# Rotated queries of the last attention turned through memory, query roots on GpSimd, and scores kept as three triangles side by side

## The reference

```python
def odd_mixer(h, w_in, q_norm_w, k_norm_w, sinks, w_out, pos):
    proj = h @ w_in
    q, k, v, gate = split(proj)            # 2048, 256, 256, 2048 columns
    q = rope(rms_norm_2(q as 32 heads of 64, q_norm_w), pos)
    k = rope(rms_norm_2(k as 4 heads of 64, k_norm_w), pos)
    o = swa_sinks(q, k, v, sinks)
    return (o * silu(gate)) @ w_out

def swa_sinks(...):                        # block = window = 128 tokens
    scores = q . k / 8                     # a block of queries sees its own and the previous block of keys
    band = (key <= query) & (query - key < 128)
    m = max(max(scores in the band), sink)
    p = exp(scores - m);  p = p / (sum(p) + exp(sink - m))
    return p @ v
```

## Time and profile before

| | |
|---|---|
| median of three runs | 1881.83 us |
| the profiled execution, its own time | 1880.64 us |
| its span | 1878.8 us |
| TensorE busy in the span | 1873.9 us (100%) |
| VectorE, ScalarE, GpSimd busy | 1255.8 us, 996.6 us, 14.4 us |
| granted clock of TensorE | 1.00 over the span |
| mean of the DMA | 200 GB/s |

### The profile page before, as it was taken

One profiled execution on the slowest core, in us unless ns is written; L12 is line 12 of the kernel. 1 busy time (PEld: TensorE's weight loads), 2 busy tenths in 40 slices (PEclk: granted clock), 3 DMA queues, 4 the chain that ended last, 5 costly groups with the idle time before them and its releaser, 6 DMA issues.

```text
span 1878.8 us, 22394 instructions
## 1 busy us (share of the span) xinstructions
PE 1873.9 (100%) x8531; PEld 1543.7 (82%) x8531; DVE 1255.8 (67%) x1837; ACT 996.6 (53%) x1370; POOL 14.4 (1%) x32
## 2 busy tenths in 40 slices
PE   9999999999999999999999999999999999999999
PEld 7888888888888888888888888888888888877777
DVE  6676566776666556665466776765776666778875
ACT  6677554554444344443444455564565555566763
POOL 0001000000000000000000000000000000000000
PEclk9999999999999999999999999999999999999999
DMA  9767764786666666666666696666666577656555
GB/s 320 207 196 176 207 183 150 217 254 195 193 193 193 195 192 191 191 199 192 191 196 193 207 280 196 193 191 190 191 200 194 194 239 236 183 160 186 174 186 178
DMA packets 212363, 375.96 MB, mean 200 GB/s; under 512 B 14673, under 2 KB 35969, under 8 KB 212257
## 3 DMA queue, kind: packets, MB, share of 16 engines
q1 hardware_dynamic: 211008, 371.78, 65.3%
q0 software_dynamic: 816, 2.11, 0.9%
q10 hardware_dynamic: 432, 0.66, 0.1%
HBM read 361.89 MB, written 12.60 MB: 199 GB/s over the span
## 4 chain that ended last, share of the span: by engine, by line
PE 100%; DVE 0%; issue 0%; DVEq 0%
PE g L1223 32%; PE g L1225 32%; PE g L1224 32%; PE m L1157 1%; PE ob L1302 0%; PE m L1284 0%; PE m L1384 0%; PE m L1282 0%; PE m L1165 0%; PE ob L1305 0%; PE m L1269 0%; PE ob L1370 0%; PE m L1314 0%; PE m L1335 0%; PE g L1211 0%; PE g L1210 0%
## 5 line engine op out<-in xcount | busy, mean ns | idle before, releaser
L1694 DVE TENSOR_TENSOR wl<-raw,wh 128x1024 fp32r<-128x1024 f32 (+1 forms) x660 | 802.3, 1217 | 544.9 <-ACT wh L1414 542.0
L1414 ACT ACTIVATE wh<-raw 128x1024 fp32r<-128x1024 f32 (+1 forms) x661 | 695.0, 1053 | 717.3 <-PE g L1225 709.5
L1223 PE MATMUL g<-wh,xh 128*128 128x512 f32 x1886 | 740.9, 393 | 0.1
L1225 PE MATMUL g<-wh,xl 128*128 128x512 f32 x1886 | 734.5, 389 | 0.0
L1224 PE MATMUL g<-wl,xh 128*128 128x512 f32 x1886 | 734.1, 389 | 0.0
L1223 PEld LDWEIGHTS g<-wh,xh 128*128 128x128 f32 x1886 | 354.1, 188 | 78.1 <-issue 3.9
L1225 PEld LDWEIGHTS g<-wh,xl 128*128 128x128 f32 x1886 | 354.0, 188 | 74.2
L1224 PEld LDWEIGHTS g<-wl,xh 128*128 128x128 f32 x1886 | 354.2, 188 | 72.1
L1223 PE MATMUL g<-wh,mh 128*128 128x512 f32 x732 | 287.6, 393 | 0.0
L1225 PE MATMUL g<-wh,ml 128*128 128x512 f32 x732 | 285.1, 389 | 0.0
L1224 PE MATMUL g<-wl,mh 128*128 128x512 f32 x732 | 284.9, 389 | 0.0
(11 more groups left out here) (186 smaller groups left out, 757.5 us busy)
## 6 DMA issues: line engine op xcount, KB each, us to landing
raw<-in_ev_w_in SPq DMA_DIRECT2D x128, 512.0 KB, 3.9
raw<-in_w_in SPq DMA_DIRECT2D x92, 512.0 KB, 4.3
raw<-in_w_gate SPq DMA_DIRECT2D x88, 512.0 KB, 4.5
raw<-in_w_up SPq DMA_DIRECT2D x88, 512.0 KB, 4.4
raw<-in_w_down SPq DMA_DIRECT2D x88, 512.0 KB, 4.7
raw<-in_od_w_in SPq DMA_DIRECT2D x72, 512.0 KB, 4.2
raw<-in_w_out SPq DMA_DIRECT2D x32, 512.0 KB, 4.2
raw<-in_ev_w_out SPq DMA_DIRECT2D x32, 512.0 KB, 4.7
```

Of the source, the lines that this page charges most:

```text
L1223: e.matmul(o, hi[:, kt, c], h, start=first, stop=False)
L1225: last = e.matmul(o, lo[:, kt, c], h, start=False, stop=end)
L1414: return e.activation(o, i, AF.Copy, scale=scale)
L1694: return e.tensor_tensor(o, a, b, op)
```

## The change

1. **Queries through memory.** `oq_turn` is gone. In its place stand `turn`, `send` and `fetch` of `("qsent", j, k)`: VectorE transposes `T3[:, k]` (128x512) in blocks of 32x32, SyncE's queue writes it with four DMAs and reads it back with four more, each 128 partitions of four runs of 32 numbers, straight into `qo`. `oqk` waits on TensorE for both fetches.
2. **Query roots on GpSimd.** `on_root j` is 14 instructions of 128x16 on GpSimd; `omax` waits for them.
3. **Three triangles.** The scores of a head keep their 384 columns. VectorE adds a band of 384 columns in one instruction; the maximum is two reductions in place of one; the second exponential has 256 columns; `oapt g 2` turns the third part of all four heads, so there are 12 transposes a group in place of 8, and nothing is taken apart behind them.
4. **Costs and order.** The table `WORK`, the gates of the lanes (`og` waits until an `ogate` is placed) and so the order from the keys of this layer on.

```diff
-        "oqk": (0, 2.9, 1.75), "omax": (0, 1.6, 0), "oexp": (1.17, 0, 0), "oapt": (.62, .84, .45), "oapv": (.6, 0, 1.6),
+        "oqk": (0, 2.2, 1.75), "omax": (0, 2.25, 0), "oexp": (1.28, 0, 0), "oapt": (.62, 0, .45), "oapv": (.6, 0, 1.6),
...
-            for k, p in enumerate(("on_sum", "on_root")):
-                yield 2 if k else 1
-                yield from self.made("on_rope", a[0], k)
-                say("oq_turn", a[0], k)
+                if k:
+                    self.sent_in_place(a[0], 0)
+            yield 1
+            yield from self.room("dve", 1.0)
+            self.sent_in_place(a[0], 1)
+            for p in ("on_sum", "on_root"):
+                yield 1
                 yield from self.room("dve", 1.0)
                 say(p, a[0])
...
+    def sent_in_place(self, j, k):
+
+        p = ("qsent", j, k)
+        self.say("turn", *p)
+        self.say("send", *p)
+        self.place[p], self.before[p] = ("q", 0), None
+        self.turns.append(p)
+        self.spawn(self.fetched_in_place(p))
+
+    def fetched_in_place(self, p):
+
+        yield 4
+        self.say("fetch", *p)
+        self.end[("fetch",) + p] = self.now + 4.6
+        yield 1
...
                 elif kind == "oqk":
                     g, j = a[0], a[0] // 2
-                    on.wait_ge(*moved("oq_turn", j, 1))
+                    for k in range(2):
+                        on.wait_ge(*back(("qsent", j, k)))
...
-                    tiles = [(h, c) for h in (2 * i, 2 * i + 1) for c in range(2)]
+                    tiles = [(h, c) for h in (2 * i, 2 * i + 1) for c in range(2)] if i < 2 else [(h, 2) for h in range(4)]
...
-                    for kb in range(2):
-                        c = od_probs(g)[:, i, 128 * kb:128 * kb + 128]
-                        last = e.activation(c, c, AF.Exp, bias=mx[:, h, kb:kb + 1],
...
+                    for kb, (lo, hi) in enumerate(((0, 128), (128, 384))):
+                        last = e.activation(od_probs(g)[:, i, lo:hi], od_probs(g)[:, i, lo:hi], AF.Exp, bias=mx[:, h, kb:kb + 1],
...
-                            own[i] = steps.mark(tt(od_probs(g)[:, i, :], od_bank(g, i)[:, 0:256], C("band", 0, 256), ALU.add))
...
-                            e.copy_predicated(od_probs(g)[:, n, 128:256], C("band", 256, 384).bitcast(i32),
-                                              od_bank(g, n)[:, 256:384]).then_inc(s_bank_dve if n < 3 else s_ob_dve, 1)
...
+                        tt(od_probs(g)[:, i, :], od_bank(g, i)[:, 0:384], C("band"), ALU.add).then_inc(s_bank_dve if i < 3 else s_ob_dve, 1)
...
-                    on.wait_ge(s_root, roots[("on_root", g // 2)])
+                    on.wait_ge(s_qroot, g // 2 + 1)
...
-                    stt(PO[2][:, 256 * i:256 * i + 256].rearrange("p (h t) -> p h t", h=2), both, -1.0, low, ALU.mult,
-                        ALU.mult)
-                    stt(both, low, 1.0, both, ALU.add, ALU.mult).then_inc(s_masked, 1)
...
+                elif kind == "on_root" and a[0] != "k":
+                    on.wait_ge(s_on_sum, nth(*p))
+                    if a[0]:
+                        on.wait_ge(s_qroot, a[0])
+                    yi = py_.bitcast(i32)
+                    on.wait_ge(*steps.mark(e.tensor_scalar(pv_, rsq[a[0]], 64e-6, None, ALU.add)))
...
+                    rows_ = memory[n % 4].rearrange("p (i n) -> p i n", i=4)
+                    if a[0] == "qsent":
+                        for i in range(4):
+                            e.dma_start(to[:, :, 32 * i:32 * i + 32], rows_[:, i].rearrange("p (m n) -> p m n", m=4)
+                                        ).then_inc(s_fetch[n % 4], 16)
```

More of the change, by code:

```diff
@@ L187, in say @@
         self.end[p] = max(self.through[x] for x, n in (("act", act), ("dve", dve)) if n) if act + dve else self.now
+        if p[0] == "on_root" and p[1] != "k":
+            self.end[p] = max(self.end[("on_sum", p[1])], self.now) + 4.2
         if p[0] in ("xturn", "mix", "hmix", "cmix", "xsent", "msent"):
@@ L419, in after @@
             assert kind == "og"
+            while a[0] >= 2 and ("ogate", 2 * a[0] - 3) not in self.said:
+                yield 1
             yield from self.room("act", .6)
@@ L506, in od_heads @@
         for g in (2 * j, 2 * j + 1):
-            while g >= 2 and ("oapt", g - 2, 1) not in self.said:
+            while g >= 2 and ("oapt", g - 2, 2) not in self.said:
                 yield 1
@@ L513, in od_quad @@
         say = self.say
+        while ("fetch", "qsent", g // 2, 1) not in self.said:
+            yield 1
         for _ in range(8):
-            if (all(self.end[p] <= self.now for p in [("oq_turn", g // 2, 1)] + self.ring[-3:] +
+            if (all(self.end[p] <= self.now for p in [("fetch", "qsent", g // 2, 1)] + self.ring[-3:] +
                     [self.ob] * (g > 0)) and
@@ L536, in od_quad @@
         yield 1
-        yield from self.made("oapt", g, 1)
+        say("oapt", g, 2)
+        yield 1
+        yield from self.made("oapt", g, 2)
         while g >= 2 and ("msent", "M5", 2 * g - 4, "o", g - 2) not in self.said:
@@ L723, in program @@
     sents = {p: n + 1 for n, p in enumerate(q for q in plan.order if q[0] in ("xsent", "msent"))}
-    assert plan.turns == [q[1:] for q in plan.order if q[0] == "turn"] == list(sents)
+    assert plan.turns == [q[1:] for q in plan.order if q[0] == "turn"]
+    assert [p for p in plan.turns if p[0] != "qsent"] == list(sents)
+    turned_n = {p: n + 1 for n, p in enumerate(plan.turns)}
     ropes = {p: n + 1 for n, p in enumerate(q for q in plan.order if q[0] == "eq_rope")}
@@ L1050, in sent @@
         def sent(p):
-            n = sents[p] - 1
+            n = turned_n[p] - 1
             return s_send[n % 2], 64 * (n // 2 + 1)
         def back(p):
-            n = sents[p] - 1
-            return s_fetch[n % 4], 16 * (n // 4 + 1)
+            n = turned_n[p] - 1
+            return s_fetch[n % 4], sum(64 if q[0] == "qsent" else 16 for q in plan.turns[n % 4:n + 1:4])
         def last_sent(*start):
@@ L1278, in tensor @@
                             on.wait_ge(*bank_free("oqk", g, n))
-                        heads = [(od_bank(g, n), qo[rows_of(n), j % 2, 2 * (g % 2) + n // 2, :],
+                        heads = [(od_bank(g, n), [qo[rows_of(n), j % 2, k, 2 * (g % 2) + n // 2] for k in range(2)],
                                   ko[rows_of(n), j, :]) for n in (i, i + 1)]
                         for o, q, k in heads:
-                            e.matmul(o[:, 0:128], q[:, 0:128], k[:, 0:128], start=True, stop=True)
+                            e.matmul(o[:, 0:128], q[0], k[:, 0:128], start=True, stop=True)
                         for n, (o, q, k) in enumerate(heads):
-                            e.matmul(o[:, 128:384], q[:, 128:256], k[:, 0:256], start=True,
+                            e.matmul(o[:, 128:384], q[1], k[:, 0:256], start=True,
                                      stop=True).then_inc(s_pv if i + n == 3 else s_bank, 1)
@@ L2232, in gpsimd @@
                     e.memset(K.rearrange("p (c t) -> p c t", t=128)[:, :, 0:1], 0.0).then_inc(s_g_one, 1)
+                elif kind == "on_root" and a[0] != "k":
[4 more added lines that the diff above has]
+                    on.wait_ge(*steps.mark(e.tensor_scalar(pv_, rsq[a[0]], 64e-6, None, ALU.add)))
+                    on.wait_ge(*steps.mark(e.tensor_scalar(yi, pv_.bitcast(i32), -0.5, 1597463007.0, ALU.mult, ALU.add)))
+                    for i in range(3):
+                        on.wait_ge(*steps.mark(e.tensor_tensor(pq_, pv_, py_, ALU.mult)))
+                        on.wait_ge(*steps.mark(e.tensor_tensor(pq_, pq_, py_, ALU.mult)))
+                        half, more = (-0.5, 1.5) if i == 2 else (-0.5, 1.5)
+                        on.wait_ge(*steps.mark(e.tensor_scalar(pq_, pq_, half, more, ALU.mult, ALU.add)))
+                        if i < 2:
+                            on.wait_ge(*steps.mark(e.tensor_tensor(py_, py_, pq_, ALU.mult)))
+                    e.tensor_tensor(rsq[a[0]], py_, pq_, ALU.mult).then_inc(s_qroot, 1)
                 elif kind == "dec":
```

117 lines of the change are left out of this document (49 added, 68 removed).

## The result

| | before | the change |
|---|---|---|
| median of 14 runs each, side by side | 1881.03 us | 1885.61 us |
| lowest and highest | 1880.32 to 1882.14 | 1883.30 to 1887.24 |
| the profiled execution, its own time | 1880.64 us | 1883.64 us |
| its span | 1878.8 us | 1881.8 us |
| VectorE, ScalarE, GpSimd busy | 1255.8, 996.6, 14.4 us | 1243.5, 999.9, 35.2 us |

The ratio is 1.0025, 95% interval 1.0018 to 1.0032: slower by 4.6 us, a little beyond the 0.2% that the prediction named. One thing must be known to read the profile: its execution ran at a mean granted clock of 1.000, as only two of the fourteen did (1883.64 and 1883.30 us). The other twelve had 0.998 or 0.999 and took 1885.04 to 1887.24.

A forecast was written before the change was run, and what follows sets the result against it. The prediction took TensorE alone, busy 50.00 of 50 us, to bound the kernel. TensorE's work summed to 0 and the fetch stall to 1.5 us, so 1881.8 + 1.5 = 1883.3 us, range 1880.8 to 1887.8.

The forecast's parts named there:

- TensorE's own work: Last attention: eight turns of queries go, eight of probabilities come, 0.44 us each, 3.5 us either way; sum 0.
- VectorE, costed at 0: Last attention: about 18 us less work on an engine off the path; at most it removes 1.0 us of waits.
- The sum of -18: VectorE's net: -13.4 for the groups, -9.9 for four roots gone, +5.7 for eight block transposes.
- ScalarE: Last attention: 32 exponentials double from 128 columns, about 0.1 us each, 3 us over 200; nothing on the path.
- GpSimd's root: 14 instructions ahead of a group's maximum take 2.5 to 11 us, hidden behind five units of 13.6 us.
- The way of the queries through memory: First scores wait for the fetched queries of block 0: a stall of 1.3 us, rounded to 1.5, bounds 0 to 8.0.
- T: Start of the unit ahead of which the second block transpose of block 0 stands; TensorE reaches the first scores at T + 10.9.
- The fetch's term: Block 0's fetch issues four DMAs until T + 7.7, after the send has landed at T + 6.0.
- The relief alone: Rival: the fetch lands in time and VectorE's relief takes the 1.0 us of waits, 1880.8 us; chance 0.15.
- The slower one: Rival at the first scores: short runs make the first fetch late, 6.5 us, so 1888.3 us; chance 0.12.
- Late splits in the new order: Rival throughout the stage: tightly placed steps make splits late and TensorE waits, 1886.8 us; chance 0.05.
- the transposes are really gone: Rival: third turns hide beside other work, TensorE keeps 3.5 us, 1879.8 with the stall, 1878.3 without; chance 0.02.

The follow-up runs named there:

- The change without its gap: The changed kernel with one edit in the order, the first scores (oqk 0) two units (5.44 us) later on every engine: 1880.76 us, ratio 1.0002.
- the fastest one: The change with two triangles in one square of scores as before, and the first scores two units later: 1876.71 us, ratio 0.9979 against the kernel before.

## Why the prediction was right, and where not

The range of 1880.8 to 1887.8 held the time, but the median, 1885.6, lies in its upper part and on the slower side of 0.2%, which had 0.17. The forecast of 1883.3 was met by the executions at full clock (1883.3 and 1883.6), and that is in part luck: it was a median of three runs, 1881.8, plus 1.5, and fourteen runs gave 1881.0. As a loss the forecast was 1.5 us; the measured one is 4.6, and 2.3 to 2.6 at full clock. What the prediction had right is the mechanism, one gap ahead of the first scores that the fetch ends; its size it had too small.

*TensorE's own work, costed at 0: right.* The change without its gap takes 1880.76 us beside 1880.67. Both halves are seen singly: eight turns of queries brought back cost 4.3 us with 0.5 more of waits in it, eight third turns taken out gain 4.05 with 0.4 of waits in it. That is 0.46 to 0.48 us a turn. From the kernel before to the fastest one it is eight turns of queries and 4.1 us, 0.51 each. So 0.44 is about right, if a little low.

*VectorE, costed at 0: right for the kernel before, wrong as a statement on the new order.* The sizes held one by one: 0.550 for 384 columns (0.416 + 0.14 put), 0.668 for the half reduction (0.6 put). The sum of -18 was too large: busy time fell by 12.3 us. A root's 2.5 us was taken from first start to last end, gaps between its instructions included; busy it is (195.24 - 187.71) / 4 = 1.9 us. That takes the sum to -15; where the other 3 us lie is open. And the cover went with the change: the planner had laid the order with a root that costs VectorE nothing, so that four roots of 2 us brought back at those places cost 4.5 us. The relief was worth 0 where it was added to the old order; under the new order it was not. With the cost told to the planner 3.7 us of it stayed, so that it is the order alone is not shown.

*ScalarE: right.* 999.9 against 996.6 busy, +3.3; 128 columns more take 0.589 against 0.483.

*GpSimd's root: right.* Here is the one of block 0, in part (columns as in TensorE's timeline):

```profile
1627.69 1.15 POOL L2236 TENSOR_SCALAR st<-st 128x16 int32<-128x16 int32 x1
1628.93 0.22 POOL L2238 TENSOR_TENSOR st<-st 128x16 f32<-128x16 f32 x1
...
1630.43 1.15 POOL L2239 TENSOR_TENSOR st<-st 128x16 f32<-128x16 f32 x1
...
1634.21 1.07 POOL L2244 TENSOR_TENSOR st<-st 128x16 f32<-128x16 f32 x1
```

VectorE's splits there ran from 1627.55 to 1628.78 and from 1630.27 to 1631.50. An instruction takes 0.2 us by itself, and 1.07 to 1.15 when it begins beside a split, ending just behind it; beside VectorE's shorter additions of 128x512 three more take 0.5 to 0.6. The whole root runs from 1627.35 to 1635.28, 7.9 us, between the bounds of 2.5 and 11. That is the exclusion which the Trainium skill (SBUF — State Buffer, "SBUF: two separate sides") describes, and by the count that the prediction made: few splits in the span, so few long instructions. Between 1600 and 1850 no engine waited for a root.

*The way of the queries through memory: the mechanism right, its size wrong by one term and one omission.* TensorE came at T + 11.0 as worked out (T + 10.9), and the block transpose was done at T + 1.5 to the tenth (T is 1623.5 here). Then:

| | predicted | measured |
|---|---|---|
| send issued until | T + 3.2 | T + 4.1 |
| fetch issued until | T + 7.7 | T + 11.1 |
| from there to the scores | 4.5 | 3.0 |
| stall | 1.3 | 3.1 |

The fetch's term is 3.4 us short. The working let the second fetch start when its send had landed, and put 0.2 us (1.3 rounded to 1.5) for loads in the same queue. In the row stand the four DMAs of the first fetch, 2.11 us, and behind them a load of 2.03 us, which no row of before could show. The landing was then too dear by 1.5, which by luck hid nearly half of the error. The omission is the clock: nothing in the sum or the rivals asked what TensorE's speed is after an idle stretch. It costs nothing in 4 of 23 executions of the change, and some 1 to 3 us in the others.

*The rivals.* The relief alone is what comes out when the gap is taken away, 1880.8. The slower one was right about its cause, short pieces that make the first fetch late, but not about its road: it priced them on the way to landing (6.8 us needed), where they took 4.0, and not in the issue of what stands behind them. The rule of the Trainium skill that was left open (DMA: Bandwidth & Descriptors, "Specifications": below 512 bytes the engine reads, changes and writes) would, as the prediction took it, have moved the time towards 1888. The measurement decides against such a size on the way to landing: with 512-byte pieces it is 3.5 us, with 128-byte pieces 4.0. Whether the rule is what holds up the issue isn't shown. Late splits in the new order did not come (0.3 us in all); the 0.4 us that matmuls wait there for another engine are for ScalarE's exponentials ahead of a turn of probabilities. That the transposes are really gone is true only of the version with one square of scores.

## What to carry to other kernels

When two parts of a change have opposite signs on the bounding engine, try each alone: here the queries' way through memory gained 4 us, the triangles gave them back, and one wait of 3 us made the sum slower. When a path from engine to memory and back is priced, write down the whole issuing queue in order with the DMAs' shapes, since what stands in front costs more than the flight; and give the consumer two units more, which costs nothing if other work fills them. Time in which TensorE idles can be paid a second time through its clock: a wait of 3 us on an otherwise full engine should be priced at 3 to 6 (one of 6.0 cost 8, those of 2.0 and 1.3 nothing more).

## What the runs showed of the hardware

- Behind a fetch of four DMAs with 512 pieces of 128 bytes each, the next DMA in the queue took 2.03 us to issue (1.89 to 2.51 in four other traces with the same order of the queue); behind four with 128 pieces of 512 bytes each, 0.44.
- TensorE idle for 3.1 to 3.2 us in the two traced executions of the change: mean clock below 1.000 in 19 of 23, with products 0.43 us apart until 6.1 us after the first score in the one traced. With 6.0 us idle in the traced one: in all 4. With 2.0 and 1.3 us: in none of 10 and 10.
- A GpSimd instruction of 128x16 took 0.20 to 0.26 us by itself and 1.07 to 1.15 when it began beside a VectorE split of 1.22 to 1.23.
